# GpSimd's powers of the S5 poles behind the convolution, ScalarE's power tables moved with them

## The chip, the cores and the metric

The kernel runs on one core of a Trainium2 chip. The metric is device time in microseconds (us) of one execution, lower is better. Five engines of the core matter here: TensorE (PE in the profile, its weight loads PEld), VectorE (DVE), ScalarE (ACT), GpSimd (POOL) and SyncE (SP), which issues most of the weight loads from HBM. Each engine takes its instructions in program order; engines wait for each other on named semaphores.

## The reference, cut to what matters

Two transformer blocks run over one sequence of 256 tokens, width 1024. The part that the change touches lies in the first block and in a preparation for the second.

```
# first block
proj = rms_norm(x) @ w_in                 # q, k, v and the 2*512 columns of the convolution
attn = attention(q, k, v)                 # 8 heads of 64, causal
conv = silu(layer_norm(causal_depthwise_conv(a * sigmoid(g))))     # 31 taps, 512 channels
x = x + concat([attn, conv]) @ w_out
h = rms_norm(x)
x = x + (silu(h @ w_gate) * (h @ w_up)) @ w_down

# second block, S5 mixer: parameters only, nothing of x
a = exp(lam * dt)                          # complex poles, 64 groups x 64 states
z = (a - 1) / lam
bb = z * b                                 # input factor
y  = scan of  state = a * state + bb @ u   # chunks of the sequence
```

The kernel does the scan in chunks of T = 8 tokens and so needs the powers a^0 to a^8 and z*a^0 to z*a^7 for each of 64 states and 64 groups. From them it builds matrices for all 64 groups. Both depend on the parameters alone, so they can be made anywhere before their use.

## The kernel before, in words

Weights come as "units" of 128 x 2048 fp32 values. SyncE loads a unit to `wraw`; ScalarE rounds it to a high part (`split_high`, L416); VectorE subtracts to make the low part (`split_low`, L422, or in two halves `low_half`, L429); TensorE multiplies high by high, high by low and low by high. Activations are split the same way (`actH`, `actL`). Some units have a place of their own in memory that is otherwise something else: unit 14 (the first gate/up unit of the first feed-forward) has its high part in `early_gain`, which is the memory of the small S5 vectors (`s_zr`, `s_zi`, `s_lamdt` and others) that GpSimd computes with.

The order on every engine is written out by hand, and waits are on semaphore counts. The stages around the change:

1. **Convolution beside the first attention.** VectorE does 76 of the taps one after another (`cacc`, L2396) between the row maxima of the heads (L1133); TensorE does the rest of the taps (L1650, L1659) between the matmuls of the heads (L1064, L1074, L1083). The last VectorE step signals `conv_done` (L2464).
2. **Layer norm of the convolution.** TensorE sums (L1669, L1676), GpSimd makes the reciprocal deviation (`pool_rstd`, "ln", L752 and L755), VectorE puts it on a diagonal (`diag`, L2489), TensorE spreads it (L1682), VectorE scales (`ln_normed`, L2494), ScalarE applies SiLU and rounds (L2098, L2093), VectorE makes the low part and signals `conv_low` (L2499). Meanwhile TensorE multiplies the four `w_out` units (L519): units 10 and 11 need only the attention, units 12 and 13 need `conv_low` 1 to 4.
3. **Into the feed-forward.** VectorE adds the product to x (`residual`, L2513, signal `f1_x_ready`), TensorE turns rows of x (`pe_row_turn`, L630), ScalarE and VectorE split them (`act_row_turn` L639, `dve_row_turn` L646), TensorE multiplies units 14 and 15 row by row (L490 to L492), then `pe_prep(0)` (L1020, L1025) uses block 0 of the S5 matrices, then the pairs of units follow, each with a gated product turned (L848) and a `pe_prep`. SiLU of the first pair (L879) waits for the reciprocal norm `rx` that GpSimd makes (L752, L755).

GpSimd's work there: `pool_s5_powers` (L1256 to L1273) makes the powers AR, AI from 54 us on, signals `powers`; `pool_s5_input_powers` waits for `conv_done`, makes the factor z (`pool_s5_input_factor`, twelve small operations, L1351 to L1360), multiplies (`cmul`, ZR and ZI, 128x512) with the layer norm's `pool_rstd` between its four products and its two sums, and signals `input_powers`. After that `pool_prep(b)` (L992, L1002, L1010) builds block b of the matrices; it waits for all eight tables (`tables_a` 8).

ScalarE's copies of the powers into the layout of the matrices are the eight `power_tables` (L2066): F1 and F2 from the powers, G1 and G2 from the input powers. Three of the F copies stand between heads 3, 4 and 5, the other five behind unit 14's `split_high`:

```
            act.wait_ge(*m.past("input_powers", 1))
            power_tables(3, 8)
            m.act_row_turn(act, "f1", ROWS_LOW, 0, range(4), N2)
            m.split_high(act, 15)
```

Of the kernel before, what the change touches and what calls it, by code (L numbers as in the profile page):

```python
# [36 lines left out]
AW = H1 * HD  # L37
# [7 lines left out]
ROWS_LOW, ROWS_HIGH = (0, 1, 2, 3), (4, 5, 6, 7)  # L45
# [1317 lines left out]
def pool_s5_powers(m, c, pool):  # L1363

    powers(c, pool, m.AR, m.AI, (m.small["ar"][:], m.small["ai"][:]), m.atmp, m.atmp2, T + 1)
    pool.memset(m.zero1[:], 0.0).then_inc(m.sem("powers"), 1)


def pool_s5_input_powers(m, c, pool):

    pool.wait_ge(*m.past("conv_done", 1))
    pool_s5_input_factor(m, c, pool)
    z = [m.small[n][:].unsqueeze(2).to_broadcast([P, NG, T]) for n in ("zr", "zi")]
    cmul(c, pool, (m.ZR[:], m.ZI[:]), (m.AR[:, :, 0:T], m.AI[:, :, 0:T]), z, (m.atmp[:], m.atmp2[:]),
         lambda: (m.pool_rstd(pool, "ln", AW, "ln_head_sums", 2), pool.wait_ge(*m.past("ln_normed", 2))))
    pool.memset(m.zero1[:], 0.0).then_inc(m.sem("input_powers"), 1)


# [63 lines left out]
N1, N2, MIXPRE, FFNPRE, GLUB, DWB, LNG, LNB, SKIP, FOXQ, FOXK = 0, 8, 16, 32, 48, 56, 60, 64, 68, 76, 77  # L1442
# [13 lines left out]
def build(nc, io, out):  # L1456
    with ExitStack() as ctx:
# [67 lines left out]
        def _(pool):  # L1525
# [23 lines left out]
            pool_s5_den(m, c, pool)  # L1549
            m.pool_rstd(pool, "k", HD, "k_head_sums", 16, m.rsk)  # L1550
            pool_s5_growth(m, c, pool)
            pool_s5_powers(m, c, pool)
            pool_s5_input_powers(m, c, pool)
            pool.wait_ge(*m.past("conv_low", 4))
            pool.wait_ge(*m.past("conv_tensor", 2))
# [414 lines left out]
        def _(act):  # L1970
# [92 lines left out]
            def power_tables(i, j):  # L2063

                for out, src, sign in s5_power_tables(m)[i:j]:
                    act.activation(out, src, ACT.Copy, scale=sign).then_inc(sem("tables_a"), 1)  # L2066

            for h in range(H1):
                if h > 0:
                    m.act_probs_turned(act, "a1", h - 1, m.pt1, (6, 7))  # L2070
                m.act_attention(act, "a1", h, m.p1, rsum, nmax, (4, 5))
                if h == 0:
                    tap_diagonals(3)
                if h == 1:
                    m.split_high(act, 11)
                for i in DIAGONALS_AT.get(h, ()):
                    shared_diagonals(i)
                if h == H1 - 1:
                    m.act_probs_turned(act, "a1", h, m.pt1, (6, 7))
                if 3 <= h < 6:  # L2080
                    act.wait_ge(*m.past("powers", 1))
                    power_tables(h - 3, h - 2)
            act.wait_ge(*m.past("a1_scores", H1))
            m.split_high(act, 12)
            m.act_turn(act, "ao", (0, 1, 2), n=4)
            act.wait_ge(*m.past("ln_centred", 1))
            act.activation(m.csq[:], m.cacc[:], ACT.Square).then_inc(sem("ln_sq"), 1)
            act.activation(m.nmax[:, 0, 0:1], m.halfpi[:], ACT.Silu)
            act.wait_ge(*m.past("ln_sq_sum", 1))

            def cv_high(j):
# [3 lines left out]
            for half in range(2):  # L2095
                act.wait_ge(*m.past("ln_normed", half + 1))
                for j in (2 * half, 2 * half + 1):
                    act.activation(m.csq[:, j, :], m.cacc[:, j, :], ACT.Silu, scale=m.vec[:, LNG + j:LNG + j + 1],  # L2098
                                   bias=m.vec[:, LNB + j:LNB + j + 1]).then_inc(sem("cv_silu"), 1)
                cv_high(2 * half)  # L2100
                cv_high(2 * half + 1)
                m.split_high(act, 13 + half)
            act.wait_ge(*m.past("input_powers", 1))
            power_tables(3, 8)
            m.act_row_turn(act, "f1", ROWS_LOW, 0, range(4), N2)
            m.split_high(act, 15)
            m.act_row_turn(act, "f1", ROWS_LOW, 1, range(4), N2)
            m.act_row_turn(act, "f1", ROWS_LOW, 0, (4, 5), N2)
            m.split_high(act, 16)
# [719 lines left out]
```

## Time and profile before

| | |
|---|---|
| median of 3 runs | 976.51 us (976.35 to 976.56) |
| the profiled execution: its time | 976.7 us |
| its span, first to last instruction | 975.0 us |
| TensorE busy | 958.6 us, 98% of the span |
| VectorE busy | 581.4 us, 60% |
| ScalarE busy | 508.0 us, 52% |
| GpSimd busy | 311.0 us, 32% |
| mean granted TensorE clock | 0.998 of full speed |

The profiled execution is one run, and its span is 1.7 us shorter than its own time, for what lies around the first and last instruction. Engine times in the sections below are microseconds from the start of its span. A view that groups instructions gives busy time and the mean of one; a timeline gives the start, the duration, and in square brackets how long the engine was idle before and which instruction released it. An instruction's start to the next one's start on the same engine is its cost there; durations overlap by a few hundredths.

### The profile page before, as it was taken

Reading aid. Unit: us, or ns where it says so; the run is one execution under the profiler, and the core shown is the slowest. Engines: PE = TensorE matmul, PEld = TensorE weight load, DVE = VectorE, ACT = ScalarE, POOL = GpSimd, SP = SyncE. Lnnn points to the kernel's source line nnn. Section 1 sums busy time; section 2 is a strip of 40 time slices with the busy share of each in tenths; the row PEclk is TensorE's granted clock in tenths of the full one; section 3 lists DMA queues with packets and bytes.
Section 4 is the critical chain, followed back from the end, with each engine's and each line's share of the span. In section 5 each row is a group of like instructions: output and inputs, shape, how many; then the busy total and the mean of one; then the engine's idle time right before and its main releaser. Section 6 shows DMA issues by size and latency. Waiting matters only on the chain.

```text
span 975.0 us, 14270 instructions
## 1 busy us (share of the span) xinstructions
PE 958.6 (98%) x5438; PEld 800.9 (82%) x5438; DVE 581.4 (60%) x634; ACT 508.0 (52%) x728; POOL 311.0 (32%) x333
## 2 busy tenths in 40 slices
PE   8999999999999999999999999999989999999997
PEld 6988788888888888888888888888969888888886
DVE  4899774555554566565755544536586765455444
ACT  5876474444443466545664444434466564444432
POOL 6680549998688127760020000000000010000000
PEclk9999999999999999999999999999999999999999
DMA  9742047777867666545366657558936365567541
GB/s 334 261 157 87 1 130 227 227 226 224 271 227 227 187 220 190 173 133 173 106 195 190 197 172 251 179 184 270 399 121 221 126 200 189 172 182 248 175 170 43
DMA packets 133828, 186.79 MB, mean 192 GB/s; under 512 B 5905, under 2 KB 104721, under 8 KB 133265
## 3 DMA queue, kind: packets, MB, share of 16 engines
q1 hardware_dynamic: 109632, 158.28, 50.1%
q10 hardware_dynamic: 24144, 27.81, 8.3%
q8 instruction: 35, 0.57, 0.2%
q14 instruction: 17, 0.13, 0.0%
HBM read 174.54 MB, written 15.73 MB: 195 GB/s over the span
## 4 chain that ended last, share of the span: by engine, by line
PE 94%; DVE 3%; ACT 1%; issue 1%; DMA 1%; POOL 0%; DVEq 0%; POOLq 0%; SPq 0%; ACTq 0%
PE ps L519 25%; PE ps L490 17%; PE ps L492 16%; PE ps L491 16%; PE ps L470 2%; PE ps L1064 2%; PE ps L472 2%; PE ps L471 2%; PE ps L848 1%; PE ps L1650 1%; PE ps L1083 1%; PE ps L1074 1%; PE ps L630 1%; PE ps L1168 1%; PE ps L1020 1%
## 5 line engine op out<-in xcount | busy, mean ns | idle before, releaser
L422 DVE TENSOR_TENSOR wlo<-wraw,whi 128x2048 fp32r<-128x2048 f32 x127 | 302.4, 2383 | 290.9 <-ACT whi L416 290.9
L416 ACT ACTIVATE whi<-wraw 128x2048 fp32r<-128x2048 f32 x127 | 243.3, 1916 | 254.3 <-PE ps L492 159.6
L490 PE MATMUL ps<-whi,actH 128*128 128x512 f32 x640 | 257.6, 402 | 1.0 <-ACT qa L2150 0.6
L492 PE MATMUL ps<-whi,actL 128*128 128x512 f32 x640 | 250.2, 391 | 0.0
L491 PE MATMUL ps<-wlo,actH 128*128 128x512 f32 x640 | 249.4, 390 | 0.0
L490 PEld LDWEIGHTS ps<-whi,actH 128*128 128x128 f32 x640 | 120.3, 188 | 27.7 <-issue 2.1
L492 PEld LDWEIGHTS ps<-whi,actL 128*128 128x128 f32 x640 | 120.1, 188 | 26.1
L765 POOL TENSOR_SCALAR ss<-ss 128x1 f32<-128x1 f32 x8 | 1.8, 221 | 436.0 <-ACT sg L735 436.0
L491 PEld LDWEIGHTS ps<-wlo,actH 128*128 128x128 f32 x640 | 120.5, 188 | 22.5
L519 PE MATMUL ps<-whi,gH 128*128 128x512 f32 x248 | 77.8, 393 | 0.0
L519 PE MATMUL ps<-wlo,gH 128*128 128x512 f32 x248 | 76.8, 390 | 0.0
L519 PE MATMUL ps<-whi,gL 128*128 128x512 f32 x248 | 76.8, 389 | 0.0
L519 PEld LDWEIGHTS ps<-whi,gL 128*128 128x128 f32 x248 | 46.6, 188 | 9.8
L519 PEld LDWEIGHTS ps<-wlo,gH 128*128 128x128 f32 x248 | 46.6, 188 | 9.8
L519 PEld LDWEIGHTS ps<-whi,gH 128*128 128x128 f32 x248 | 45.9, 188 | 10.2 <-issue 1.2
L470 PE MATMUL ps<-actH,whi 128*128 128x256 f32 x160 | 45.6, 285 | 0.2 <-DVE wlo L422 0.2
L471 PE MATMUL ps<-actL,whi 128*128 128x256 f32 x160 | 45.3, 283 | 0.0
L472 PE MATMUL ps<-actH,wlo 128*128 128x256 f32 x160 | 45.3, 283 | 0.0
L886 ACT ACTIVATE gH<-ps 128x512 f32 (+1 forms) x33 | 19.8, 599 | 42.5 <-PE ps L848 42.5
L1114 ACT ACTIVATE p<-ps,nmax 128x128 f32<-128x128 f32 (+1 forms) x48 | 19.7, 417 | 36.5 <-DVE nmax L1133 36.5
L2396 DVE SCALAR_TENSOR_TENSOR cacc<-hpad,vectors,cacc 128x256 f32<-128x256 f32 x76 | 35.0, 529 | 0.3 <-ACT cacc L2042 0.3
L1010 POOL TENSOR_TENSOR ob<-ob,otmp 128x576 f32<-128x576 f32 x16 | 32.7, 2045 | 1.3
(453 smaller groups left out, 1571.0 us busy)
## 6 DMA issues: line engine op xcount, KB each, us to landing
wraw<-in_ffn_w_gate SPq DMA_DIRECT2D x44, 512.0 KB, 4.0
wraw<-in_ffn_w_up SPq DMA_DIRECT2D x44, 512.0 KB, 5.0
wraw<-in_ffn_w_down SPq DMA_DIRECT2D x18, 1024.0 KB, 4.9
wraw<-in_fox_w_in SPq DMA_DIRECT2D x16, 1024.0 KB, 5.5
wraw<-in_w_gate SPq DMA_DIRECT2D x22, 512.0 KB, 4.0
wraw<-in_w_up SPq DMA_DIRECT2D x22, 512.0 KB, 5.0
wraw<-in_w_in SPq DMA_DIRECT2D x9, 1024.0 KB, 10.9
wraw<-in_w_down SPq DMA_DIRECT2D x9, 1024.0 KB, 5.1
```

The costliest lines, as they stand in the source:

```text
L416: act.activation(self.high_of(n0), self.wraw[:, n0 % RAW, :], ACT.Copy).then_inc(self.hi_done, 1)
L422: dve.tensor_tensor(self.low_of(n0), self.wraw[:, n0 % RAW, :], self.high_of(n0).bitcast(F32), ALU.subtract).then_inc(self.lo_done, 1)
L470: pe.matmul(out, wh, self.actH[:, k, :], start=(i == 0), stop=False)
L471: pe.matmul(out, wh, self.actL[:, k, :], start=False, stop=False)
L472: last = pe.matmul(out, wl, self.actH[:, k, :], start=False, stop=(i == KT - 1))
L490: pe.matmul(out, xh, wh, start=(ka == 0), stop=False)
L491: pe.matmul(out, xh, wl, start=False, stop=False)
L492: last = pe.matmul(out, xl, wh, start=False, stop=(ka == KT - 1))
L519: last = pe.matmul(self.ps[:, base + 2 * r + c, :], x, w[c], start=st, stop=sp_)
L886: act.activation(self.g_tiles(self.gH, f, f_step), self.ps[:, self.turn_bank(f0, at_end), :].rearrange("p (a b) -> p a b", a=2), ACT.Copy)\
L1010: pool.tensor_tensor(o, o, t[:], ALU.add).then_inc(done, 1)
L2396: steps[j] = c.step(dve.scalar_tensor_tensor(m.cacc[:, j, :], src, w, m.cacc[:, j, :], ALU.mult, ALU.add))
```

## The change

GpSimd's `pool_s5_powers` moves behind the wait for `conv_done`. The layer norm's `pool_rstd` follows it, ahead of the input factor, instead of standing inside the product. A second signal of `powers` follows the four products that read the small S5 vectors. ScalarE makes three F tables behind the layer norm's square instead of between the heads, waits for the second `powers` ahead of unit 14's `split_high`, and makes the other five tables behind unit 15's `split_high` and row 0's turn instead of ahead of both.

```diff
 def pool_s5_input_powers(m, c, pool):
 
     pool.wait_ge(*m.past("conv_done", 1))
+    pool_s5_powers(m, c, pool)
+    m.pool_rstd(pool, "ln", AW, "ln_head_sums", 2)
     pool_s5_input_factor(m, c, pool)
     z = [m.small[n][:].unsqueeze(2).to_broadcast([P, NG, T]) for n in ("zr", "zi")]
     cmul(c, pool, (m.ZR[:], m.ZI[:]), (m.AR[:, :, 0:T], m.AI[:, :, 0:T]), z, (m.atmp[:], m.atmp2[:]),
-         lambda: (m.pool_rstd(pool, "ln", AW, "ln_head_sums", 2), pool.wait_ge(*m.past("ln_normed", 2))))
+         lambda: (c.wait(), pool.memset(m.zero1[:], 0.0).then_inc(m.sem("powers"), 1),
+                 pool.wait_ge(*m.past("ln_normed", 2))))
     pool.memset(m.zero1[:], 0.0).then_inc(m.sem("input_powers"), 1)
...
             pool_s5_growth(m, c, pool)
-            pool_s5_powers(m, c, pool)
             pool_s5_input_powers(m, c, pool)
...
                 if h == H1 - 1:
                     m.act_probs_turned(act, "a1", h, m.pt1, (6, 7))
-                if 3 <= h < 6:
-                    act.wait_ge(*m.past("powers", 1))
-                    power_tables(h - 3, h - 2)
...
             act.activation(m.nmax[:, 0, 0:1], m.halfpi[:], ACT.Silu)
+            act.wait_ge(*m.past("powers", 1))
+            power_tables(0, 3)
             act.wait_ge(*m.past("ln_sq_sum", 1))
...
                 cv_high(2 * half + 1)
+                if half:
+                    act.wait_ge(*m.past("powers", 2))
                 m.split_high(act, 13 + half)
+            m.act_row_turn(act, "f1", ROWS_LOW, 0, range(4), N2)
+            m.split_high(act, 15)
             act.wait_ge(*m.past("input_powers", 1))
             power_tables(3, 8)
-            m.act_row_turn(act, "f1", ROWS_LOW, 0, range(4), N2)
-            m.split_high(act, 15)
             m.act_row_turn(act, "f1", ROWS_LOW, 1, range(4), N2)
```

How it moves GpSimd's instructions behind the convolution. Before, from the last memset of the powers on:

```order
L1366 MEMSET zero_68 128x1 [waits pool_chain]
L1351 TENSOR_TENSOR s_nre<-s_em,cosT 128x64 [waits conv_done]
L1360 TENSOR_TENSOR s_zi<-s_zi,s_rden 128x64 [waits pool_chain]
L1256 TENSOR_TENSOR ZR<-AR,s_zr 128x512 [waits pool_chain]
L1259 TENSOR_TENSOR atmp_97<-AI,s_zr 128x512
L752 TENSOR_SCALAR rs<-ss 128x2 [waits all_head_sums]
L755 TENSOR_TENSOR rs<-rs,mhalf 128x2 [waits all_var]
L1263 TENSOR_TENSOR ZR<-ZR,atmp 128x512 [waits pool_chain,ln_normed]
```

In the changed kernel, from the first instruction behind `conv_done` on (of the powers and of the factor the first and the last stand here):

```order
L1270 MEMSET AR 128x64 [waits conv_done,pool_chain]
L1264 TENSOR_TENSOR AI<-AI,atmp_97 128x64x4
L1366 MEMSET zero_68 128x1 [waits pool_chain]
L752 TENSOR_SCALAR rs<-ss 128x2 [waits all_head_sums]
L755 TENSOR_TENSOR rs<-rs,mhalf 128x2 [waits all_var]
L1351 TENSOR_TENSOR s_nre<-s_em,cosT 128x64
L1360 TENSOR_TENSOR s_zi<-s_zi,s_rden 128x64 [waits pool_chain]
L1256 TENSOR_TENSOR ZR<-AR,s_zr 128x512 [waits pool_chain]
L1259 TENSOR_TENSOR atmp_97<-AI,s_zr 128x512
L1377 MEMSET zero_68 128x1 [waits pool_chain]
L1263 TENSOR_TENSOR ZR<-ZR,atmp 128x512 [waits pool_chain,ln_normed]
```

The 22 operations of the powers now stand between `conv_done` and the layer norm's two operations, and the factor with its four products stands behind those two.

ScalarE from the second half of SiLU to row 1's turn, before:

```order
L2093 ACTIVATE actH<-csq 128x256 [waits cv_silu] x2
L416 ACTIVATE early_gain<-wraw 128x2048 [waits raw_landed2]
L2066 ACTIVATE F_84<-AR 64x576 [waits input_powers]
L2066 ACTIVATE G_85<-ZR 64x512
L2066 ACTIVATE G_85<-ZI 64x512
L2066 ACTIVATE G_86<-ZI 64x512
L2066 ACTIVATE G_86<-ZR 64x512
L639 ACTIVATE actH<-ps,vectors 128x128 [waits all_transposed] x2
L639 ACTIVATE actH<-ps,vectors 128x128 [waits all_act_ready,all_transposed] x2
L416 ACTIVATE early_nat<-wraw 128x2048 [waits raw_landed3]
```

In the changed kernel:

```order
L2094 ACTIVATE actH<-csq 128x256 [waits cv_silu] x2
L416 ACTIVATE early_gain<-wraw 128x2048 [waits raw_landed2,powers]
L639 ACTIVATE actH<-ps,vectors 128x128 [waits all_transposed] x2
L639 ACTIVATE actH<-ps,vectors 128x128 [waits all_act_ready,all_transposed] x2
L416 ACTIVATE early_nat<-wraw 128x2048 [waits raw_landed3]
L2068 ACTIVATE F_84<-AR 64x576 [waits input_powers]
L2068 ACTIVATE G_85<-ZR 64x512
L2068 ACTIVATE G_85<-ZI 64x512
L2068 ACTIVATE G_86<-ZI 64x512
L2068 ACTIVATE G_86<-ZR 64x512
```

Unit 14's high part (`early_gain`) has a new wait for GpSimd, and the five tables stand between unit 15's high part (`early_nat`) and row 1's turn. Lines of the changed kernel are up to three numbers higher than the same lines before.

## Rows read from the trace of the kernel before

**Rows 1.** The page: busy time and share of each engine

```profile
PE 958.6 (98%) x5438; PEld 800.9 (82%) x5438; DVE 581.4 (60%) x634; ACT 508.0 (52%) x728; POOL 311.0 (32%) x333
```

**Rows 2.** Windows: us, busy of PE, PEld, DVE, ACT, POOL, clock, DMA

```profile
87.00:105.00 18.00, 17.72 (x111) 15.34 (x111) 17.68 (x48) 12.33 (x41) 0.21 (x1) 1.00 0.18 58
```

**Rows 3.** Groups by form, VectorE's taps at 57.4 to 71.3, then 71.5 to 103

```profile
L2396 DVE SCALAR_TENSOR_TENSOR cacc<-hpad,vectors,cacc 128x256 f32<-128x256 f32 x16 | 10.7, 735 | 0.3 <-ACT cacc L2042 0.3
...
L2396 DVE SCALAR_TENSOR_TENSOR cacc<-hpad,vectors,cacc 128x256 f32<-128x256 f32 x59 | 24.0, 474 | 0.0
```

**Rows 4.** Timeline of POOL: start, duration, what, idle before and releaser

```profile
54.08 0.22 POOL L1270 MEMSET AR<- 128x64 f32 x1
...
70.45 0.10 POOL L1366 MEMSET zero<- 128x1 f32 x1
104.79 0.32 POOL L1351 TENSOR_TENSOR s_nre<-s_em,cosT 128x64 f32<-128x64 f32 x1 [34.24 <-DVE cacc L2464]
...
109.28 1.09 POOL L1256 TENSOR_TENSOR ZR<-AR,s_zr 128x512 f32<-128x512 f32 x1
```

**Rows 5.** Timeline of POOL, the layer norm and the sums of the product

```profile
113.92 2.16 POOL L752 TENSOR_SCALAR rs<-ss 128x2 f32<-128x2 f32 x1 [0.43 <-DVE ss L2484]
116.17 0.72 POOL L755 TENSOR_TENSOR rs<-rs,mhalf 128x2 f32<-128x2 f32 x1
...
120.96 1.48 POOL L1264 TENSOR_TENSOR ZI<-ZI,atmp 128x512 f32<-128x512 f32 x1
```

**Rows 6.** Timeline of DVE, the layer norm and the low parts

```profile
113.75 2.28 DVE L422 TENSOR_TENSOR wrawlow<-wraw,early_qt 128x2048 fp32r<-128x2048 f32 x1
...
120.58 2.15 DVE L2499 TENSOR_TENSOR actL<-csq,actH 128x256 fp32r<-128x256 f32 x2 [0.94 <-ACT actH L2093]
123.13 2.29 DVE L422 TENSOR_TENSOR wlo<-wraw,whi 128x2048 fp32r<-128x2048 f32 x1 [0.41 <-ACT whi L416]
...
126.54 2.29 DVE L422 TENSOR_TENSOR wrawlow<-wraw,early_gain 128x2048 fp32r<-128x2048 f32 x1 [0.44 <-ACT early_gain L416]
130.00 1.28 DVE L2513 TENSOR_TENSOR x_res<-x_res,ps 128x512 f32<-128x512 f32 x2 [1.17 <-PE ps L519]
```

**Rows 7.** Timeline of ACT, from SiLU to the first pair

```profile
119.14 1.10 ACT L2098 ACTIVATE csq<-cacc,vectors 128x256 f32<-128x256 f32 x2 [6.71 <-DVE cacc L2494]
...
124.60 1.91 ACT L416 ACTIVATE early_gain<-wraw 128x2048 fp32r<-128x2048 f32 x1
126.53 0.69 ACT L2066 ACTIVATE F<-AR 64x576 f32<-64x576 f32 x1
...
135.45 0.63 ACT L639 ACTIVATE actH<-ps,vectors 128x128 fp32r<-128x128 f32 x2 [0.36 <-PE ps L630]
...
150.04 0.84 ACT L879 ACTIVATE sg<-ps,rx 128x256 f32<-128x256 f32 x2 [2.90 <-POOL rx L755]
...
153.04 1.92 ACT L416 ACTIVATE whi<-wraw 128x2048 fp32r<-128x2048 f32 x1 [1.50 <-PE ps L492]
```

**Rows 8.** Timeline of PE, at the places where the change reaches it

```profile
121.43 0.70 PE L519 MATMUL ps<-early_qt,actH 128*128 128x512 f32 x2 [0.34 <-DVE actL L2499]
...
131.16 0.60 PE L630 MATMUL ps<-ident,x_res 128*128 128x128 f32 x4
...
136.64 0.40 PE L490 MATMUL ps<-early_gain,actH 128*128 128x512 f32 x1
...
145.50 0.60 PE L1020 MATMUL ps<-ident,rtb 128*128 128x128 f32 x4
...
158.91 0.50 PE L490 MATMUL ps<-whi,actH 128*128 128x512 f32 x1
```

**Rows 9.** Timeline of POOL, block 0 and the norm of the feed-forward

```profile
129.98 0.35 POOL L1561 MEMSET ksb<- 128x128 f32 x2 [7.38 <-ACT G L2066]
...
136.08 1.45 POOL L1010 TENSOR_TENSOR ob<-ob,otmp 128x576 f32<-128x576 f32 x1
...
149.45 0.56 POOL L755 TENSOR_TENSOR rx<-rx,mhalf 128x1 f32<-128x1 f32 x1
```

**Rows 10.** Timeline of PE, its first matmuls

```profile
3.95 3.59 PE L578 MATMUL ps<-identb 128*128 128x512 bf16 x8 [3.95 <-POOL zero L1248]
```

## The prediction

> **What bounds the kernel now.** I read the page first: TensorE is busy 958.6 of 975.0 us [rows 1], so a change pays only where TensorE waits, and costs wherever it makes TensorE wait. Second, a window over the attention that the change relieves: in the last 18 us beside the convolution VectorE has 17.68 busy, but TensorE also 17.72 [rows 2]. Both are full, and TensorE waits 0.28 us in all. So VectorE may be late there without TensorE noticing. Third, the timelines of the four engines from the end of the convolution (104.7) to the second pair of the feed-forward (159), since every moved instruction lands there. Here the engines hand over to each other with almost nothing to spare: TensorE waits 0.34 us for the layer norm's low part [rows 8]; VectorE waits only 1.17 us before the residual [rows 6]; ScalarE waits 0.36 us before row 1's turn and 1.50 before unit 18 [rows 7]. GpSimd alone had room, and the change fills it.
>
> One behaviour of the trace decides the case. A GpSimd operation on two columns takes 2.16 us when it comes 0.17 us after the start of a VectorE low part (L422, 2.28 us, both inputs in SBUF), and ends with it [rows 5, 6]. The other way round, two low parts L2499 take 2.15 us together while GpSimd's sum of 1.48 runs [rows 5, 6]. VectorE's taps took 0.735 us each beside the powers and 0.474 without [rows 3]. So such a VectorE operation and a GpSimd operation exclude each other, one waiting for the other's end. GpSimd's four products at 109.28 took 1.09 each [rows 4], since VectorE then had only work with one operand in PSUM.
>
> **The change part by part.**
>
> *Powers away from the taps.* VectorE gets back 16 x (0.735 - 0.474) = 4.2 us [rows 3]. I give TensorE nothing for it: it follows its own pace there [rows 2], so VectorE will wait for scores instead; `conv_done` can come some tenths earlier, no more. Three F tables (0.69 each) leave the heads and go where ScalarE waits 6.71 us for the layer norm [rows 7]: nothing, as long as the powers are ready by 117.0.
>
> *Powers ahead of the layer norm.* Beside the taps they took 70.45 + 0.10 - 54.08 = 16.5 us [rows 4]. Unhindered I estimate: twelve 64-column operations of the factor took 109.28 - 104.79 = 4.5 us, 0.37 each with their waits [rows 4], a 512-column product 1.09, a sum about 1.3. Between these, ten small operations at 0.3, six of 128 columns at 0.43, six of 256 at 0.67 make 9.6 us, a little less where no wait stands between. From 104.7 they end near 114. The norm's two operations before began at 113.92, were held until 116.08 by unit 12's low part and ended at 116.9 [rows 5]. They are held by the same low part now, so most of the powers fits into time that was lost anyway. I take +0.4 us for a last sum caught in it and for VectorE's diagonal meeting the factor. Ends: 0, and 104.8 + 16.5 + 1 = 122.3 against 116.9, +5.4.
>
> *Factor and products behind the norm; unit 14 waits for them.* From 117.3: factor 4.5 us plus 1.0 in which VectorE's diagonal and two low parts pass, 122.8; products 4 x 1.05, with unit 13's low part (2.29 [rows 6]) and two more L2499 let in between, 3.0 together: 130.0 at the latest, 129.4 if one slips in earlier. ScalarE was ready for `early_gain` at 124.60 [rows 7]. It starts at 129.5 and ends at 131.3. GpSimd goes on with its two sums of 1.25, and unit 14's low part gets in between or behind them: 132.0 to 134.3, where it ended at 128.83. The residual is queued behind it on VectorE, at 134.3 instead of 130.00 [rows 6]; TensorE's first turn of x follows 0.7 later, at 135.1 instead of 131.16 [rows 8]. **TensorE +4.0** (this holds the 0.4 above).
>
> *Five tables ahead of row 1's turn.* ScalarE: row 0 and unit 15 follow the shift; then 5 tables, 0.69 + 4 x 0.63 = 3.2 us (before in a gap, now not). Row 1 began at 135.45 after 0.36 idle [rows 7], so now 135.1 + 4.0 + 3.2 = 142.3. From its start to a finished operand pair it is 0.8 us, and TensorE took that at 136.64 [rows 8], 0.4 after it was ready. 136.64 + 6.85 - 0.4: **TensorE +6.4, 2.4 more**. Ends: 0 and 3.2.
>
> *Block 0 beside unit 15's halves.* GpSimd's block 0 waits for all tables: 142.4 instead of 129.98 [rows 9]. Its six operations took 137.5 - 130.0 = 7.5 us. Now VectorE's two half low parts of unit 15, and unit 16's, fall among them, each waiting on average half an operation of 1.1 to 1.4. **+1.4**, ends 0 and 2.5. Block 0 is done near 153; TensorE asks for it at 145.50 + 7.8 = 153.3 [rows 8]: covered, barely.
>
> *The feed-forward's norm behind block 1.* GpSimd does half of block 1 (3.4 us), then `rx` (1.8), with the low parts of units 16 and 17 let in (2 x 2.3): 161 instead of 150.0 [rows 9]. ScalarE's SiLU of pair 0 waits for it, +11 [rows 7]. Its next work, unit 18's high part, moves from 153.04 to 164.1 [rows 7]; high and low take to 157.3 before, 168.4 now. TensorE wants unit 18 at 158.91 + 7.8 = 166.7 [rows 8], plus some tenths for the gated turn of pair 0: **+1.3 to +1.7**. Behind this, GpSimd is a block ahead of TensorE and the shift stays as it is.
>
> Sum: 4.0 + 2.4 + 1.4 + 1.6 = +9.4 us, on a profiled execution of 976.7 us (span 975.0 and 1.7 around it). That stands 0.2 above the median of the runs shown, so I forecast 976.5 + 9.4 = 985.9, say 986.0. What follows at 160 is bound by TensorE to the end [rows 1]; I see nothing that gives the time back.
>
> The page "SBUF — State Buffer" of the Trainium skill (Who interferes with whom, and its summary) names the exclusion, for a VectorE instruction with two SBUF inputs against a GpSimd one that reads SBUF, and advises to put whichever is off the critical path elsewhere. By that advice the taps, with VectorE busy 98% of the time, are the place to clear. Here the rows say the opposite: the place cleared had TensorE as its pace, the place filled has VectorE's low parts on the path.
>
> **The rivals.**
>
> *B, the exclusion hardly bites in the new place: +2.4 us, 978.9.* For it: how operations interleave hangs on tenths, and GpSimd's four products ran free before. Then powers and norm are on time, products end at 117 + 4.5 + 4.2 = 125.7, `early_gain` is 1.1 late, and VectorE's idle 1.17 covers it. The tables' 2.4 remain, and `rx` is inside its reserve. Against it: all of unit 12's to 17's low parts lie in the window. It decides if `early_gain` starts before 126.
>
> *C, faster: the taps were the bound.* If busy TensorE (its ends are modelled) hides waits for VectorE's row maxima, the 4.2 us given back reach the end: 972.3. It decides where TensorE's last head ends by 2 us or more earlier. Against it: after the powers end at 70.5, six heads pass at TensorE's pace with 0.28 us of waits [rows 2].
>
> *D, TensorE's clock falls, or the layer norm is hit whole.* The new wait of 4 us before x's first turn is longer than any since the start. There, after 3.95 us without work, eight matmuls of 512 columns took 3.59 us, 0.43 from one to the next [rows 10]; later the same width takes 0.23. The granted clock shows full speed in both, yet the first is the pace of 1.2 GHz and the second that of 2.4. A fall after a stall costs the same again, 8 x 0.2 = 1.6 us, perhaps twice; or the powers run past 118 and the norm is 2 or 3 late. +12 to +15, 989 to 991.
> The page "TensorE: Matmul & The Clock Gate" of the Trainium skill (Why this matters for your kernels) warns of idle gaps between bursts of matmuls, after which the engine is back at half its clock. By that rule D's first form would come true; whether 4 us suffice no row since the start shows.
>
> *E, no change:* the tables too are hidden and the norm is on time, within 1.9 us of 976.5.
>
> **How the numbers follow.** This measurement can tell about 0.2%, 1.95 us, from no change. Chances: the forecast (+6 to +12) 0.68, B 0.14, D 0.09, E 0.05, C 0.04. The forecast's own range is 983 to 988.5. The range for 8 in 10 reaches to the upper half of B's spread and into D: 980.0 to 990.0. Faster 0.04 (C), within 0.2% 0.06 (E and B's lowest end), slower 0.90.
>
> **What would show it.** Right: attention's last matmuls at the same time (within 0.5 us); taps beside 57 to 71 at 0.41 to 0.48 us; powers from 104.5 to about 114; `rs` done at 116.9 to 117.6; `early_gain` waiting for GpSimd's memset near 129.4; the residual near 134; TensorE waiting 3 to 4 us at L630 and about 2 before row 1's products; `rx` near 161; the distance of the two kernels constant from 180 on. Wrong: `early_gain` starting before 126 (B), a residual on time, a fall of the matmuls' pace behind the waits (D), `conv_done` more than 1 us earlier together with TensorE's first layer-norm matmul (C).

## The result, and the profile after

| | before | changed |
|---|---|---|
| median | 976.51 us (5 runs, 976.33 to 976.57) | 986.09 us (5 runs, 985.9 to 986.33) |
| ratio, 95% interval | | 1.0099 (1.0087 to 1.011) |
| profiled execution, its span | 976.7, 975.0 us | 986.33, 984.5 us |
| TensorE idle in the span | 975.0 - 958.6 = 16.4 us | 984.5 - 962.0 = 22.5 us |

The change is 9.6 us slower, where the forecast was 9.4 (986.0). Of the span's +9.5, 6.1 us are idle time of TensorE and 3.4 are busy time. The same matmuls were issued, so some of them are recorded longer: 1.65 us more between x's first turn and row 1's first product (7.29 us busy instead of 5.64), where the granted clock fell, and the rest in pieces of under 1 us over the other stages.

The page of the changed kernel, its line of busy times (to be held against [rows 1]):

```profile
PE 962.0 (98%) x5438; PEld 802.3 (81%) x5438; DVE 581.9 (59%) x634; ACT 508.0 (52%) x728; POOL 309.9 (31%) x334
```

**Where the change takes work away.** First the window over the attention in its columns (us, busy of PE, PEld, DVE, ACT, POOL, clock, DMA share, GB/s), then the taps at 57 to 71 by form:

```profile
87.00:105.00 18.00, 17.72 (x112) 15.35 (x109) 16.33 (x43) 8.72 (x33) 0.39 (x4) 1.00 0.11 37
```

```profile
L2399 DVE SCALAR_TENSOR_TENSOR cacc<-hpad,vectors,cacc 128x256 f32<-128x256 f32 x16 | 6.6, 481 | 0.3 <-ACT cacc L2044 0.3
```

The sixteen taps take 6.6 us instead of 10.7 [rows 3], and in the window VectorE is busy 16.33 us instead of 17.68 [rows 2]. TensorE is busy 17.72 us in both. VectorE waits for scores instead.

**Where it puts work.** GpSimd's timeline (start, duration, what, idle before and releaser), beside [rows 4, 5, 9]:

```profile
104.61 0.21 POOL L1270 MEMSET AR<- 128x64 f32 x1 [50.43 <-DVE cacc L2467]
...
114.07 2.80 POOL L1264 TENSOR_TENSOR AI<-AI,atmp 128x256 f32<-128x256 f32 x1
...
117.39 0.72 POOL L755 TENSOR_TENSOR rs<-rs,mhalf 128x2 f32<-128x2 f32 x1
...
124.97 3.13 POOL L1258 TENSOR_TENSOR ZI<-AR,s_zi 128x512 f32<-128x512 f32 x1
...
129.38 0.10 POOL L1377 MEMSET zero<- 128x1 f32 x1
...
160.39 0.56 POOL L755 TENSOR_TENSOR rx<-rx,mhalf 128x1 f32<-128x1 f32 x1
```

VectorE's timeline, beside [rows 6]:

```profile
113.91 2.34 DVE L422 TENSOR_TENSOR wrawlow<-wraw,early_qt 128x2048 fp32r<-128x2048 f32 x1
...
124.27 2.89 DVE L422 TENSOR_TENSOR wlo<-wraw,whi 128x2048 fp32r<-128x2048 f32 x1 [1.64 <-ACT whi L416]
...
131.46 2.70 DVE L422 TENSOR_TENSOR wrawlow<-wraw,early_gain 128x2048 fp32r<-128x2048 f32 x1 [1.86 <-ACT early_gain L416]
134.09 1.27 DVE L2516 TENSOR_TENSOR x_res<-x_res,ps 128x512 f32<-128x512 f32 x2
```

The two lists have to be read together. The powers' last sum starts at 114.07, 0.16 us after unit 12's low part. It ends at 116.87 instead of within a microsecond, and the norm's two operations come behind it. The third product (124.97) and unit 13's low part (124.27) meet in the same way: 3.13 us for an operation that took 1.08 just before.

ScalarE's timeline, beside [rows 7]:

```profile
129.51 1.92 ACT L416 ACTIVATE early_gain<-wraw 128x2048 fp32r<-128x2048 f32 x1 [3.67 <-POOL zero L1377]
...
142.13 0.63 ACT L639 ACTIVATE actH<-ps,vectors 128x128 fp32r<-128x128 f32 x2
```

Unit 14's high part has waited 3.67 us for GpSimd's memset, where it followed without a pause. Row 1's turn comes at 142.13 behind the five tables, where it came at 135.45.

TensorE's, beside [rows 8]:

```profile
122.32 0.70 PE L519 MATMUL ps<-early_qt,actH 128*128 128x512 f32 x2
...
134.82 0.66 PE L630 MATMUL ps<-ident,x_res 128*128 128x128 f32 x4 [1.94 <-DVE x_res L2516]
...
142.94 0.50 PE L490 MATMUL ps<-early_gain,actH 128*128 128x512 f32 x1 [0.83 <-DVE actL L646]
...
148.60 0.63 PE L630 MATMUL ps<-ident,x_res 128*128 128x128 f32 x4 [0.93 <-DVE actL L646]
153.19 0.60 PE L1020 MATMUL ps<-ident,rtb 128*128 128x128 f32 x4
...
168.41 0.47 PE L490 MATMUL ps<-whi,actH 128*128 128x512 f32 x1 [1.61 <-DVE wlo L422]
```

The difference of the starts, place by place, is the account of the loss. In the attention the matmuls of the two executions already stand 0.16 us apart. Both start TensorE at the same time (3.95 and 3.93), but the first product with weights comes at 11.38 and at 11.54: the time goes in the first matmuls, which the change doesn't touch. That much is in every row of the table, so the change itself accounts for 0.16 less in each.

| place on TensorE | before | changed | difference |
|---|---|---|---|
| unit 12's first matmul (L519) | 121.43 | 122.32 | +0.89 |
| x's first turn (L630) | 131.16 | 134.82 | +3.66 |
| row 1's first product (L490) | 136.64 | 142.94 | +6.30 |
| block 0 (L1020) | 145.50 | 153.19 | +7.69 |
| unit 18 (L490) | 158.91 | 168.41 | +9.50 |

From there to the end nothing changes any more. The windows behind unit 18, of the kernel before and of the changed one, are equally long and equally busy:

```profile
158.90:975.00 816.10, 805.29 (x4582) 671.34 (x4578) 458.50 (x436) 403.46 (x529) 220.74 (x199) 1.00 0.60 196
```

```profile
168.41:984.50 816.09, 805.29 (x4578) 671.25 (x4578) 460.14 (x437) 401.85 (x528) 221.43 (x200) 1.00 0.60 196
```

One thing I had given only a small chance happened: the granted clock fell. Windows of the changed kernel, and TensorE's matmuls in them:

```profile
136.00:138.00 2.00, 2.00 (x9) 1.65 (x8) 1.76 (x6) 1.78 (x4) 0.00 (x0) 0.56 0.01 2
138.00:140.00 2.00, 2.00 (x7) 1.57 (x7) 0.56 (x1) 1.95 (x3) 0.00 (x0) 0.59 0.04 8
```

```profile
138.35 0.63 PE L491 MATMUL ps<-wrawlow,actH 128*128 128x512 f32 x1
138.78 0.63 PE L492 MATMUL ps<-early_gain,actL 128*128 128x512 f32 x1
...
141.25 0.40 PE L490 MATMUL ps<-early_gain,actH 128*128 128x512 f32 x1
141.49 0.39 PE L491 MATMUL ps<-wrawlow,actH 128*128 128x512 f32 x1
```

At 138.35 the matmuls start 0.43 us apart, the pace of 1.2 GHz; at 141.25, where the granted clock is back at 1.00, they start 0.24 apart, that of 2.4. From x's first turn to its third it took 140.11 - 134.82 = 5.29 us, where the kernel before took 3.65: 1.6 us lost to the clock, right behind the wait of 1.94.

### The profile page after: what moved, and what is told of

It reads as the page before. It is cut to its first block, busy times and chain, and to the rows that moved or that the text cites. A ratio compares the mean times of both kernels' runs of the same rounds, so it can differ in the third digit from the quotient of the medians.

```text
span 984.5 us, 14273 instructions
## 1 busy us (share of the span) xinstructions
PE 962.0 (98%) x5438; PEld 802.3 (81%) x5438; DVE 581.9 (59%) x634; ACT 508.0 (52%) x728; POOL 309.9 (31%) x334
## 4 chain that ended last, share of the span: by engine, by line
PE 89%; POOL 5%; DVE 3%; ACT 2%; issue 1%; ACTq 0%; POOLq 0%; DVEq 0%
PE ps L519 23%; PE ps L490 16%; PE ps L492 16%; PE ps L491 16%; PE ps L470 2%; PE ps L1064 2%; PE ps L472 2%; PE ps L471 2%; PE ps L848 1%; PE ps L1652 1%; PE ps L1083 1%; PE ps L1074 1%; PE ps L1168 1%; PE ps L1661 1%; PE ps L1020 1%
## 5 line engine op out<-in xcount | busy, mean ns | idle before, releaser
L490 PE MATMUL ps<-whi,actH 128*128 128x512 f32 x640 | 257.5, 402 | 2.6 <-DVE wlo L422 1.6
L490 PEld LDWEIGHTS ps<-whi,actH 128*128 128x128 f32 x640 | 120.3, 188 | 29.2 <-issue 3.9
L491 PEld LDWEIGHTS ps<-wlo,actH 128*128 128x128 f32 x640 | 120.5, 188 | 22.5
L519 PE MATMUL ps<-whi,gH 128*128 128x512 f32 x248 | 77.8, 393 | 0.0
L519 PE MATMUL ps<-wlo,gH 128*128 128x512 f32 x248 | 76.8, 390 | 0.0
L519 PE MATMUL ps<-whi,gL 128*128 128x512 f32 x248 | 76.8, 389 | 0.0
L519 PEld LDWEIGHTS ps<-whi,gL 128*128 128x128 f32 x248 | 46.5, 188 | 9.8
L519 PEld LDWEIGHTS ps<-wlo,gH 128*128 128x128 f32 x248 | 46.5, 188 | 9.8
L519 PEld LDWEIGHTS ps<-whi,gH 128*128 128x128 f32 x248 | 45.9, 188 | 10.2 <-issue 1.2
L879 ACT ACTIVATE sg<-ps,rx 128x256 f32<-128x256 f32 x66 | 27.1, 461 | 8.3 <-POOL rx L755 8.3
L2399 DVE SCALAR_TENSOR_TENSOR cacc<-hpad,vectors,cacc 128x256 f32<-128x256 f32 x76 | 31.0, 482 | 0.3 <-ACT cacc L2044 0.3
```

Of the source, the lines that this page charges most:

```text
L490: pe.matmul(out, xh, wh, start=(ka == 0), stop=False)
L491: pe.matmul(out, xh, wl, start=False, stop=False)
L519: last = pe.matmul(self.ps[:, base + 2 * r + c, :], x, w[c], start=st, stop=sp_)
L879: act.activation(self.sg[:, 256 * r:256 * r + 256], self.ps[:, banks[r], 0:256], ACT.Silu, scale=self.rx[:, r:r + 1]).then_inc(self.sem(st ...
L2399: steps[j] = c.step(dve.scalar_tensor_tensor(m.cacc[:, j, :], src, w, m.cacc[:, j, :], ALU.mult, ALU.add))
```

## The experiments

The theory is that of the prediction: three links, each held by the exclusion of VectorE and GpSimd or by ScalarE's order. They are the layer norm and unit 14 behind the powers, the tables ahead of row 1, and the norm of the feed-forward behind block 1. In their traces the attention's matmuls stand 0.33 to 0.56 us earlier than in the changed kernel's, and as in the table above this comes from the first 12 us: TensorE starts at 3.93 to 3.95 in all of them, and its first product with weights comes at 10.98 to 11.22 instead of 11.54. Fences show times as they are; where a sentence compares two traces, it says that this is taken off.

**Powers back beside the attention, everything else as changed.**

```diff
     pool.wait_ge(*m.past("conv_done", 1))
-    pool_s5_powers(m, c, pool)
     m.pool_rstd(pool, "ln", AW, "ln_head_sums", 2)
...
             pool_s5_growth(m, c, pool)
+            pool_s5_powers(m, c, pool)
             pool_s5_input_powers(m, c, pool)
```

> The changed kernel with the powers back beside the first attention; the layer norm's two operations stay ahead of the factor, unit 14's wait and the tables' places stay. Theory A (the loss comes from the factor and the products behind the norm, from unit 14's wait for them and from the tables' place, not from where the powers are made): 984.5 to 986, the norm done at 116.9, early_gain still starting near 129, taps at 0.73 us beside the powers. Rival B (the powers behind the convolution are the cost, by making the norm late): most of the loss goes, 976.5 to 979. Rival C (the taps' freedom hides part of a larger loss): 987 to 990.

Measured: 985.41 us (984.94 to 985.5, 4 runs), ratio 1.0091 (1.0075 to 1.0108). GpSimd, ScalarE and TensorE of this kernel:

```profile
115.83 0.72 POOL L755 TENSOR_TENSOR rs<-rs,mhalf 128x2 f32<-128x2 f32 x1
```

```profile
128.00 1.92 ACT L416 ACTIVATE early_gain<-wraw 128x2048 fp32r<-128x2048 f32 x1 [3.66 <-POOL zero L1376]
```

```profile
141.44 0.50 PE L490 MATMUL ps<-early_gain,actH 128*128 128x512 f32 x1 [2.43 <-DVE actL L646]
```

The norm is on time again, and with it 0.7 us come back, no more. The title of the change names the powers, but with the rest of the change in place their own place is worth only that; the factor and the products behind the norm, and the tables' place, keep nearly all of the loss. What the powers would cost if they alone were moved no run shows. The taps are at 737 ns again, as before the change, and the time still falls. So giving VectorE its 4 us in the attention was worth nothing.

**Only the tables moved.** The kernel before, with its five tables behind unit 15's high part.

```diff
-            act.wait_ge(*m.past("input_powers", 1))
-            power_tables(3, 8)
             m.act_row_turn(act, "f1", ROWS_LOW, 0, range(4), N2)
             m.split_high(act, 15)
+            act.wait_ge(*m.past("input_powers", 1))
+            power_tables(3, 8)
             m.act_row_turn(act, "f1", ROWS_LOW, 1, range(4), N2)
```

> The kernel before with one thing changed: the five tables stand behind unit 15's high part instead of ahead of row 0's turn. Theory A (3.2 us ahead of row 1's turn against 0.8 of reserve, then block 0 and the feed-forward's norm late with it): 2.4 + 1.4 + 1.6 = +5.4 at most, 980 to 982.5, TensorE waiting about 2.4 before row 1's products and again at unit 18. Rival B (only the wait at row 1 counts, what follows has reserve): +2.4, 978.5 to 979.3. Rival C (ScalarE has room there and the tables' place is free): 976.5.

Measured: 982.18 us (982.01 to 982.46, 4 runs), ratio 1.0059 (1.0042 to 1.0075). TensorE of this kernel:

```profile
130.83 0.60 PE L630 MATMUL ps<-ident,x_res 128*128 128x128 f32 x4
...
138.90 0.50 PE L490 MATMUL ps<-early_gain,actH 128*128 128x512 f32 x1 [2.42 <-DVE actL L646]
...
144.57 0.63 PE L630 MATMUL ps<-ident,x_res 128*128 128x128 f32 x4 [0.93 <-DVE actL L646]
...
164.36 0.47 PE L490 MATMUL ps<-whi,actH 128*128 128x512 f32 x1 [1.59 <-DVE wlo L422]
```

x's turn is on time, and then the three waits come that this edit alone makes: 2.42 + 0.93 + 1.59 = 4.9 of its 5.7 us. Two lines of ScalarE's order, with not one instruction added, cost 0.6%.

**Only the tables left where they were.** The changed kernel, with the five tables ahead of row 0's turn.

```diff
+            act.wait_ge(*m.past("input_powers", 1))
+            power_tables(3, 8)
             m.act_row_turn(act, "f1", ROWS_LOW, 0, range(4), N2)
             m.split_high(act, 15)
-            act.wait_ge(*m.past("input_powers", 1))
-            power_tables(3, 8)
```

> The changed kernel with the five tables back ahead of row 0's turn. Behind early_gain ScalarE waited 4.08 us for TensorE's turn in the changed kernel, and the input powers are there at 132.1. Theory A (tables' place and unit 14's wait are two costs that follow each other): the first, +3.7 at x's first turn, stays, the rest mostly goes: 980.5 to 982. Rival B (one cause only, the late input powers: wherever the tables stand, row 1 and block 0 are late): 984 to 986.

Measured: 982.49 us (981.48 to 982.57, 4 runs), ratio 1.0062 (1.0045 to 1.0078). TensorE and ScalarE of this kernel:

```profile
134.49 0.66 PE L630 MATMUL ps<-ident,x_res 128*128 128x128 f32 x4 [1.94 <-DVE x_res L2516]
...
145.46 0.63 PE L630 MATMUL ps<-ident,x_res 128*128 128x128 f32 x4 [1.08 <-DVE actL L646]
```

```profile
131.88 0.68 ACT L2068 ACTIVATE F<-AR 64x576 f32<-64x576 f32 x1 [0.79 <-POOL zero L1379]
```

The tables now fill ScalarE's wait for x's turn, the waits at row 1 and at unit 18 are gone, and those at x's turn and at unit 15 remain. The profiled execution is the lowest of the four; the other three (982.48 to 982.57) lie 1.0 us above it and 0.5 above my range's end. No fall of the clock shows in its trace. One in the other three would be of the right size, but they have no trace, so this is open.

With the kernel before and the changed one, these two make a square: the tables alone cost 5.7 us, the rest alone 6.0, both together 9.6. They overlap by 2.1 us; my explanation, which is argued and not shown, is that TensorE can wait for two late things at once. The 6.0 holds the unexplained 1.0 us: by the traced execution alone the rest costs 5.0, and the overlap is 1.0.

**Unit 14 freed from the products.** The changed kernel with the eight small S5 vectors that factor and products use in memory of their own, and so without ScalarE's new wait.

```diff
-        self.lamdt = pen("s5_lamdt", [P, 3, NG])
+        kept = Pen(175200, P0)
+        self.lamdt = kept("s5_lamdt", [P, 3, NG])
...
-        self.small |= {n: pen("s5_" + n, [P, NG]) for n in
+        self.small |= {n: (kept if n in "t sh rden em ar ai nre zr zi".split() else pen)("s5_" + n, [P, NG])
...
                 cv_high(2 * half + 1)
-                if half:
-                    act.wait_ge(*m.past("powers", 2))
                 m.split_high(act, 13 + half)
```

> The changed kernel, with the small S5 vectors that the factor and the products read in memory of their own, and without ScalarE's wait for the second `powers` ahead of unit 14's high part. A (the account so far): the wait is one of two links that hold x's turn and row 1. Without it `early_gain` starts near 126 instead of 129.5, TensorE's wait at L630 falls from 1.94 to under 1 us, x's turn comes 1 to 2 us earlier (133 to 133.8); but the powers' product and the sums stay where they are, so the tables and block 0 win only part of it. Time 984.3 to 985.3, 1 to 1.8 us under the changed kernel. B (the wait is hidden by the tables, which alone set row 1): row 1 stays within 0.3 of 142.94 and the time within 0.3 of 986.1. C (the wait is the whole cause of +3.7 at x's turn): x's turn at 131.5 and the time 982 to 983.

Measured: 984.95 us (984.79 to 985.21, 4 runs), ratio 1.0087 (1.0071 to 1.0102). ScalarE, VectorE and TensorE of this kernel:

```profile
125.37 1.90 ACT L417 ACTIVATE early_gain<-wraw 128x2048 fp32r<-128x2048 f32 x1
```

```profile
129.13 3.39 DVE L423 TENSOR_TENSOR wrawlow<-wraw,early_gain 128x2048 fp32r<-128x2048 f32 x1
```

```profile
133.17 0.66 PE L631 MATMUL ps<-ident,x_res 128*128 128x128 f32 x4 [0.71 <-DVE x_res L2515]
...
141.29 0.50 PE L491 MATMUL ps<-early_gain,actH 128*128 128x512 f32 x1 [2.42 <-DVE actL L647]
```

As A said. With the 0.41 us between the traces taken off, the high part is 3.7 us earlier, but the low part only 1.9 (it was at 131.46), since GpSimd's products hold VectorE up. It then takes 3.39 us instead of 2.70, beside the sums of the product, and x's turn is 1.2 us earlier. Taking a wait off a chain gives what the next link lets through: 1.1 us of the time.

**Nine matmuls in TensorE's wait, against the fall of the clock.** The changed kernel, with nine matmuls on a spare bank in TensorE's wait for the residual.

```diff
-                           lambda: f1_turn(0, 0), lambda: f1_turn(0, 1))
+                           lambda: (m.keep_warm(pe, 0, 9), f1_turn(0, 0)), lambda: f1_turn(0, 1))
```

> The changed kernel, with nine matmuls on a spare bank ahead of x's first turn, in TensorE's wait for the residual, whose result nobody reads. A: the granted clock stays 1.00 in 136 to 140 (0.56 and 0.59 in the changed kernel) and row 0's matmuls stand 0.23 apart instead of 0.43, but what that saves, 1.6 us, is lost again in a longer wait of TensorE ahead of row 1 (2.3 to 2.6 us instead of 0.83), which hangs on ScalarE's tables. Time within 0.4 us of 986.1. B (the lower clock carries through to the end): 984.3 to 984.7. C: nine matmuls do not keep the clock, the windows read 0.56 to 0.6 as before and the time is 986 to 988.

Measured: 986.0 us (985.77 to 986.38, 4 runs), ratio 1.0097 (1.0082 to 1.0113). TensorE, and windows, of this kernel:

```profile
132.19 2.12 PE L578 MATMUL ps<-identb 128*128 128x512 bf16 x9
...
142.40 0.50 PE L490 MATMUL ps<-early_gain,actH 128*128 128x512 f32 x1 [2.41 <-DVE actL L646]
```

```profile
138.00:140.00 2.00, 1.99 (x11) 1.37 (x9) 0.02 (x1) 1.93 (x4) 0.00 (x0) 1.00 0.00 0
...
142.00:145.00 3.00, 2.60 (x8) 2.14 (x9) 2.76 (x5) 2.78 (x6) 2.92 (x4) 0.74 0.00 0
```

The clock stays at full speed where it had fallen, and TensorE is ready for row 1 1.6 us sooner, only to wait 2.41 us there instead of 0.83, since the tables set row 1's time: 142.40, with 0.56 us between the traces 142.96, against 142.94. So in the changed kernel the fallen clock cost the total nothing that shows: 986.0 against 986.09, the theory's number. What I had not expected is that a fall then comes some 6 us later, behind the longer wait (0.74 in 142 to 145). It made block 0 0.16 us late, which the wait at unit 18 took up. That it was the nine matmuls that kept the clock up is not shown: the next experiment's kernel, whose order is that of the changed one up to here, kept it without them.

**The feed-forward's norm ahead of block 1.** In the changed kernel GpSimd makes `rx` before block 1's first half.

```diff
-            m.pool_prep(pool, 1, parts=(0,))
             m.pool_rstd(pool, "f1", D, "f1_squares", out=m.rx)
+            m.pool_prep(pool, 1, parts=(0,))
             m.pool_prep(pool, 1, parts=(1,))
```

> The changed kernel, with GpSimd's reciprocal norm `rx` of the feed-forward ahead of block 1 instead of behind its first half. A (the last term of the sum is the norm that comes late): ScalarE's squares end at 154.8, `rx` is done near 156 instead of 160.95, SiLU starts near 156 and unit 18's high part near 159.5 instead of 164.02, TensorE's wait of 1.61 us at unit 18 goes, and block 1, which starts near 156 and takes 7 us, is done near 163.2, before TensorE asks for it at about 164.3. Time 984.2 to 984.9, 1.2 to 1.9 us under the changed kernel. B (block 1 becomes what TensorE waits for): a new wait ahead of L1020 near 164, time 985.5 to 987. C (the wait at unit 18 hangs on something else, TensorE's own turn or a transfer): time within 0.3 of 986.1 with the wait still there.

Measured: 985.52 us (985.32 to 985.86, 4 runs), ratio 1.0094 (1.0077 to 1.0111): 0.6 us, between A and B. GpSimd, VectorE and TensorE of this kernel:

```profile
156.62 0.56 POOL L755 TENSOR_TENSOR rx<-rx,mhalf 128x1 f32<-128x1 f32 x1
...
162.93 3.34 POOL L1010 TENSOR_TENSOR ob<-ob,otmp 128x576 f32<-128x576 f32 x1
```

```profile
162.16 2.84 DVE L422 TENSOR_TENSOR wlo<-wraw,whi 128x2048 fp32r<-128x2048 f32 x1 [3.38 <-ACT whi L416]
```

```profile
142.52 0.50 PE L490 MATMUL ps<-early_gain,actH 128*128 128x512 f32 x1 [2.42 <-DVE actL L646]
...
166.32 0.66 PE L1020 MATMUL ps<-ident,rtb 128*128 128x128 f32 x4 [0.85 <-POOL ob L1010]
```

Both came. The wait at unit 18 is gone, as A said, so `rx` was what it hung on. But block 1's last sum now meets unit 18's low part, takes 3.34 us instead of 1.43, and TensorE has a new wait of 0.85 us.

Up to GpSimd's block 1 this kernel does what the changed one does, in the same order, so its trace is a second look at the clock behind x's first turn. Its windows:

```profile
135.00:140.00 5.00, 5.00 (x27) 3.87 (x25) 2.41 (x6) 4.61 (x8) 0.00 (x0) 1.00 0.08 24
140.00:145.00 5.00, 2.58 (x9) 2.01 (x9) 2.65 (x5) 4.71 (x10) 3.09 (x5) 0.87 0.00 0
```

TensorE waited 1.93 us at x's first turn, as in the changed kernel (1.94), and the clock did not fall there. Row 1's first product came at 142.52, with the 0.44 us between the traces 142.96, against 142.94. This says the same as the nine matmuls do: without the fall TensorE waits longer (2.42 us) and row 1 is where it was. Here too the clock fell only behind that wait.

**The powers' arithmetic taken out.** In the kernel before, every product and sum of the powers becomes four memsets of the same tiles. The powers above the first are not computed; the products, tables and matrices made of them are still made, of zeros.

```diff
-        cmul(c, pool, (tr[:, :, n + 1:n + 1 + k], ti[:, :, n + 1:n + 1 + k]),
-             (tr[:, :, 1:1 + k], ti[:, :, 1:1 + k]), b, (tmp1[:, :, 0:k], tmp2[:, :, 0:k]))
+        for _ in range(6):
+            c.step(pool.memset(tmp1[:, :, 0:k], 0.0))
+            c.step(pool.memset(tmp2[:, :, 0:k], 0.0))
+            c.step(pool.memset(tr[:, :, n + 1:n + 1 + k], 0.0))
+            c.step(pool.memset(ti[:, :, n + 1:n + 1 + k], 0.0))
+            c.wait()
```

> The kernel before with the products of the powers, beside the taps, replaced by memsets of the same tiles, six rounds of four for each step; the powers are not computed. GpSimd then writes there but reads nothing. Theory A (VectorE operations with two inputs in SBUF and GpSimd operations exclude each other by GpSimd's reads; TensorE sets the pace of the attention): taps at 0.48 us beside the memsets, time 976.0 to 977.0 although VectorE has 4 us more. Rival B (any GpSimd work slows them): taps at 0.6 us and more, same time. Rival C (the taps are on the path): taps at 0.48 us and 972 to 974.

Measured: 976.44 us (976.29 to 976.67, 10 runs), ratio 0.9999 (0.999 to 1.0009). VectorE of this kernel, then GpSimd ahead of the memsets:

```profile
53.91 2.29 DVE L422 TENSOR_TENSOR wlo<-wraw,whi 128x2048 fp32r<-128x2048 f32 x1 [0.32 <-ACT whi L416]
...
62.74 4.04 DVE L2400 SCALAR_TENSOR_TENSOR cacc<-hpad,vectors,cacc 128x256 f32<-128x256 f32 x10
...
71.18 0.62 DVE L1133 TENSOR_REDUCE nmax<-ps 128x1 f32<-128x128 f32 x2 [2.20 <-PE ps L1065]
```

```profile
54.01 2.36 POOL L1272 COPY AR<-s_ar 128x64 f32<-128x64 f32 x1
```

Ten taps take 4.04 us, 0.40 from one to the next, with a GpSimd memset almost all the time; a copy of 64 columns, which reads SBUF, waits out the low part beside it in 2.36 us. What excludes is GpSimd's reading. And the time: VectorE gets its 4 us without any of the change's costs, then waits 2.20 us for scores at 71.18, and the kernel is as fast as before within 0.1%. The taps were not the bound (rival C falls).

**GpSimd's work spread the other way.** The kernel before with the factor ahead of the wait for `conv_done`, the product whole ahead of the norm, and the five tables ahead of the layer norm's square, where ScalarE idles.

```diff
-    pool.wait_ge(*m.past("conv_done", 1))
     pool_s5_input_factor(m, c, pool)
+    pool.wait_ge(*m.past("conv_done", 1))
...
-    cmul(c, pool, (m.ZR[:], m.ZI[:]), (m.AR[:, :, 0:T], m.AI[:, :, 0:T]), z, (m.atmp[:], m.atmp2[:]),
-         lambda: (m.pool_rstd(pool, "ln", AW, "ln_head_sums", 2), pool.wait_ge(*m.past("ln_normed", 2))))
+    cmul(c, pool, (m.ZR[:], m.ZI[:]), (m.AR[:, :, 0:T], m.AI[:, :, 0:T]), z, (m.atmp[:], m.atmp2[:]))
...
+    m.pool_rstd(pool, "ln", AW, "ln_head_sums", 2)
...
+            act.wait_ge(*m.past("input_powers", 1))
+            power_tables(3, 8)
...
-            act.wait_ge(*m.past("input_powers", 1))
-            power_tables(3, 8)
```

> The kernel before, with GpSimd's input factor ahead of the wait for `conv_done` (beside the taps, where GpSimd idles), the sums of the product ahead of the layer norm instead of behind, and the five tables in ScalarE's idle time ahead of the layer norm's square. A: VectorE is not the bound beside the taps (TensorE 17.72 of 18 us), so the 12 small operations cost it nothing that shows; four products and two sums take 104.8 to 112, before the norm's sums are wanted; block 0 comes early; nothing behind it waited for the factor, since TensorE has only waits of some tenths there. Time 975.9 to 976.6, not to be told from the kernel before. B (GpSimd's sums of three SBUF operands hold VectorE's work of the layer norm ahead of the path): TensorE's first matmul of unit 12 comes 1 to 3 us late, time 977.5 to 979.5. C (the taps were the bound beside the factor): 977 to 978 with TensorE's last head later.

Measured: 976.29 us (976.14 to 976.62, 11 runs) beside 976.46 of the kernel before, ratio 0.9998 (0.9989 to 1.0007). GpSimd of this kernel:

```profile
110.78 1.29 POOL L1264 TENSOR_TENSOR ZI<-ZI,atmp 128x512 f32<-128x512 f32 x1
113.97 2.16 POOL L752 TENSOR_SCALAR rs<-ss 128x2 f32<-128x2 f32 x1 [1.74 <-DVE ss L2484]
```

The product is done at 112.1 with 1.74 us to spare, 10 us before the kernel before has it, and nothing is won: nothing there waited for it. None of the versions tried here beats the kernel before by more than can be measured.

## Why the prediction was right

The total (986.0 against 986.09) is close because its terms were: +4.0, +2.4, +1.4 and +1.6 were forecast, and the table gives +3.66, +2.64, +1.39 and +1.81. Three of them hid an error each, and that these cancelled to 0.1 us is luck.

- **Powers ahead of the layer norm, +0.4:** `rs` was done at 118.1 instead of 116.9, +1.2, and TensorE's unit 12 came 0.89 late. I had the powers end near 114 and "a last sum caught". It was caught, but it ended 0.6 us after the low part, with memset and both norm operations queued behind it. The term counted the sum and forgot its queue. The factor so began at 118.08 instead of 117.3. The memset behind it still came on time, by luck: factor and products took 11.3 us, where I had given 12.1. That the norm's delay reached the end is shown by the powers put back, which gave 0.7 us.
- **Unit 14 waits for factor and products, x's turn +4.0:** +3.66. The memset came at 129.38 (forecast 129.4), the residual at 134.09 (134.3). But I wrote that TensorE would wait 3 to 4 us at L630, and it waits 1.94. TensorE itself reached the place late: its unit 13 began at 128.52, +1.44. Of that 0.89 are unit 12's, from the first error; the rest came at a wait of 0.40 us for `actL` (L2502), whose two halves took 2.52 us beside GpSimd's third product. So the lateness is split between a wait and earlier small ones.
- **Tables ahead of row 1, +6.4:** +6.30, with ScalarE at 142.13 (forecast 142.3). TensorE's wait there was to be about 2 us and is 0.83, since 1.6 us of it went into slow matmuls; in the two traces without that fall it is 2.41 and 2.42.
- **Block 0 beside unit 15's halves, +7.8 in all:** +7.69. The wait is TensorE's for unit 15's row turn, not for block 0, which was done at 151.6. VectorE's halves take 1.80 and 1.79 us instead of 1.38 and 1.21, and TensorE waits 0.93 for them.
- **`rx` behind block 1, unit 18 +1.3 to +1.7:** `rx` is done at 160.95 (161), and the wait is 1.61; unit 18's own step in the table is +1.81 (9.50 - 7.69), a little above the +1.7. The run with `rx` first shows that the wait hangs on `rx`.
- **Nothing for the taps:** right, by the powers put back and by the memsets.

Rival B fell with `early_gain` at 129.51 (it needed to be under 126). C and E fell with the result itself, C also with the memsets. **Rival D was half right.** Its second form, powers past 118 and the norm 2 or 3 late, did not come (116.87, and 1.2). The clock of its first form fell behind the wait at x's first turn to 0.56 and 0.59. The page "TensorE: Matmul & The Clock Gate" of the Trainium skill (Why this matters for your kernels) warns of idle gaps between bursts of matmuls, after which the engine is back at half its clock. The trace agrees that the clock falls behind a wait, but the waits here (1.94 to 2.43 us) are shorter than the gaps the page warns of, and not every one brought a fall. On D's time of 989 to 991 no trace agrees. D's step that failed is "costs the same again": I added the slow matmuls to the path, but the path at that moment ran through ScalarE's tables, and the 1.6 us fell into a wait that was there anyway (row 1 at 142.94, and at 142.96 in both traces without the fall).

On the exclusion, the run with memsets adds what the trace of before could not show: ten taps beside memsets take 4.04 us, 0.40 each, while sixteen beside the products took 10.7, 0.67 each [rows 3]. That is the rule of the page "SBUF — State Buffer" of the Trainium skill (Who interferes with whom), that a VectorE instruction with two SBUF inputs contends with GpSimd instructions that read SBUF and not with those that only write it. It also sets two sentences of mine right. GpSimd's four products at 109.28 ran free not only beside operations with one operand in PSUM: from 110.95 on VectorE reduced `csq` (L2482), one input in SBUF, for 2.02 us. And the advice in that page's summary goes by what is off the critical path, where I read it by the busy share. VectorE was 98% busy beside the taps, yet freeing it changed nothing (976.44 us with the memsets), so it was off the path there, and the rows don't say the opposite of the page.

## What to carry to other kernels

GpSimd work that reads SBUF costs VectorE time wherever VectorE has two inputs in SBUF. Put it where VectorE has slack towards the pace-setting engine, even if VectorE looks 98% busy there, and not where it and the pace-setter hand over to each other. Cost a moved step by all that its queue holds back: here the five copies on ScalarE, moved by two lines, were worth more than the 22 operations that gave the change its name. When several waits are late together, undoing them one at a time shows each at less than its worth (3.6, 0.7, 1.1 and 0.6 us, together 6.0 of 9.6), because what one gives back another takes; a square of runs, each alone and both, shows the overlap.

## What was new about the hardware

**The clock falls behind short waits, not always.** In the changed kernel it fell after a wait of 1.94 us (0.56 in 136 to 138). Three more traces have that wait at x's first turn, and no fall behind it: 1.97 us with the powers back, 1.94 with the tables early, 1.93 with `rx` first. Row 1's wait was 2.41 to 2.43 us in five traces. The clock fell behind it in three: with the powers back (0.69 in 140 to 145), with the nine matmuls (0.74 in 142 to 145) and with `rx` first (0.87 in 140 to 145). It did not with only the tables moved, nor with memory of its own. What decides is not shown by these runs, and with one trace of each kernel it is not known either whether the next execution of the same kernel falls in the same place. All these waits are shorter than the 3.95 us at the start that I had argued from.

**Both engines pay.** The sum at 114.07 is recorded with 2.80 us, of which 0.6 are behind the end of VectorE's low part. But the low parts get longer too: 2.89 us instead of 2.29 for unit 13's, beside two products. Where operations of both engines stand in a row, they take turns.
